# Dividing the attention shares of two mixing layers on ScalarE instead of GpSimd

## The chip, the cores and the metric

The kernel runs on one core of one Trainium2 chip. The metric is the device time of one execution in microseconds (us), the median of several executions; lower is better. A core has TensorE (PE in the profile, its weight loads apart as PEld), VectorE (DVE), ScalarE (ACT), GpSimd (POOL) and SyncE (SP), each with its own in-order instruction stream; they meet at semaphores.

## The reference, cut to what matters

Two transformer blocks run one after the other on 256 tokens of width 1024, all in float32. The second block prepends 16 meta tokens (272 rows in all) and has two layers; each has a mixing part with an attention branch and a convolution branch, then a feed-forward part. The attention branch is what the change touches:

```python
def sink_softmax(s, sink):
    m = jnp.maximum(jnp.max(s, -1, keepdims=True), sink)
    p = jnp.exp(s - m)
    return p / (jnp.sum(p, -1, keepdims=True) + jnp.exp(sink - m))
# one head: scores of a tile of queries, plus a bias table, masked
# p = sink_softmax(concat(s_meta, s_band), sink); o = p @ v
...
# the other branch, from the same projection u of the layer's input
h = val * sigmoid(gate); h = causal depthwise conv of width 31 (h) + db
y_conv = silu(layer_norm(h)) @ w_conv_proj
mix = (sigmoid(u_ga) * (attention @ w_attn_proj) + sigmoid(u_gc) * y_conv) @ w_out
```

There are 8 query heads of 64 and 2 key heads, a window of 128, and an attention sink per head. The "shares" are `p` after the division by its row sum.

## The kernel before, in words

Weights stream from HBM as 308 units of 16 tiles of 128x128. SyncE issues their loads into a ring of four staging buffers (`stg`). ScalarE rounds a unit to a high part (`wh`, line 1239), VectorE subtracts to get the low part (`wl`, line 1745); both rings hold three units. A matrix product is three matmuls per tile: high by high, high by low, low by high (lines 538 to 540 for tiles of 272 or 256 columns). The splits are written into the ScalarE and VectorE streams at each unit's boundary, for the unit two ahead.

Each engine's program is one Python function (`tensor_program`, `scalar_program`, `vector_program`, `gpsimd_program`, `sync_program`), and each has its own `mix_layer(l)` for the two mixing layers l = 0 and 1. In that stage TensorE computes 30 column tiles `nt` of the input projection (`u` and `g`), one after the other, 24 matmuls each. The evacuation of a tile is `evac(nt)` on ScalarE and VectorE; on TensorE, `pump(nt)` stands behind the tile's matmuls. From `nt` = 13 on (`FIRST_STEP`) every `evac` and `pump` also carries two steps of the attention. A job is one head and one tile of queries: 24 jobs in layer 0, in turns of two jobs of 16 queries and 16 keys, two of 128 queries and 144 keys, two of 128 and 272; 16 jobs in layer 1, without the 16-query ones. Step i of an engine does, where the job exists:

- TensorE (`pump`, `step`): for even i the product of shares and values of jobs i-8 and i-7 (`values`, line 819, which waits for `turned_p` of job i-7); for even i the scores of jobs i and i+1 (line 835); then the transposes of the shares of job i-5 (line 845, `DEEP` = 5), which wait for the shares of that job.
- VectorE (`front`, `back`): `front` adds the bias to the scores in PSUM, takes the maximum with the sink and writes the logits to one of five SBUF buffers `L` (line 2084). It also waits until job i-5, which had that buffer, is transposed. `front` of both jobs comes first, then three taps of the convolution (line 2109), then `back` of both jobs, the reciprocal of the row sum (line 2091), which waits for the exponential; then the rest of the taps due and, at a unit's boundary, the split.
- ScalarE (`step`): copies the transposed shares of job i-5 from PSUM to SBUF (line 1484), then the exponential of job i in place, with its row sum (line 1491), and, for every last job of a pair of heads, the high part of the attention output (lines 1498 and 1499).
- GpSimd (`step`): waits for the reciprocal of job i and multiplies the job's `L` by it, in place (line 2589).

So the order of the work is written out by hand, an order per engine; nothing is planned at run time. The taps of the convolution must all be done before TensorE sums them (`conv_sums`, line 881), which it does after the first tile of the attention's output projection. Then a layer norm over the convolution and an activation run through VectorE and ScalarE, before the next projection can end.

PSUM has eight banks, handed out in turn; a bank is used again once what was in it has been read.

Of the kernel before, what the change touches and what calls it, by code (L numbers as in the profile page):

```python
# [11 lines left out]
ALU = mybir.AluOpType  # L12
ACT = mybir.ActivationFunctionType
# [4 lines left out]
KD = D // P  # L18
# [141 lines left out]
DEEP = 5  # L160
BEHIND = DEEP + 2
FIRST_STEP = 13
# [29 lines left out]
def model_kernel(nc, first_d, w_d, x_d, meta_d, small_d, const_d, look_d, out_d):  # L192
# [3 lines left out]
    with ctx:  # L196
# [10 lines left out]
        m = Marks(handle)  # L207
# [46 lines left out]
        for l in range(2):  # L254
            c = MIXER[l]
            with ExitStack() as st:
# [3 lines left out]
                    TH=sb(f"TH{l}", [P, c["HT"], S], F32R, st), TL=sb(f"TL{l}", [P, c["HT"], S], F32R, st),  # L260
                    L=[sb(f"Lm{l}{i}", [P, c["NK"]], F32, st) for i in range(c["ring"] - 1)] + [flat(XC)[:, 1024:1024 + c["NK"]]],
                    PT=[sb(f"PTm{l}{i}", [P, c["NCH"], P], F32, st) for i in range(2)]
                    + [flat(SQ)[:, 1024:1024 + c["NCH"] * P].rearrange("p (c n) -> p c n", n=P)],
                    z=sb(f"zm{l}", [P, c["ring"] + 2, 8], F32, st)))
# [3 lines left out]
        for l in range(2):  # L268
            with ExitStack() as st:
                both = sb(f"H{l}", [P, 32, 2, S], F32R, st)  # L270
                ffn.append(dict(H=both, HH=both[:, :, 0, :], HL=both[:, :, 1, :],
                                t=[sb(f"ft{l}{i}", [P, S], F32, st) for i in range(3)], u=[sb(f"fu{l}{i}", [P, S], F32, st) for i in range(3)]))
        mix2 = []
        for l in range(2):
            with ExitStack() as st:
# [4 lines left out]
                    SG=sb(f"SG{l}", [P, 2, KD, T], F32, st), MH=sb(f"MH{l}", [P, KD, T], F32R, st), ML=sb(f"ML{l}", [P, KD, T], F32R, st),  # L280
                    ns=sb(f"ns{l}", [P, 8], F32, st), L=[sb(f"Lb{l}{i}", [P, T + 1], F32, st) for i in range(DEEP)],
                    PT=[sb(f"PTb{l}{i}", [P, 3, P], F32, st) for i in range(3)], z=sb(f"zb{l}", [P, DEEP + 2, 8], F32, st)))
# [104 lines left out]
        JOBS2 = [band_jobs(0), band_jobs(1)]  # L387
# [26 lines left out]
        def tensor_program(w, pe):  # L414
# [205 lines left out]
            def turn_pair(tag, a, i, j, last):  # L620
# [3 lines left out]
                for g in range(0, len(ch), 4):  # L624
# [3 lines left out]
                    for c, (k, wide, _) in enumerate(four):  # L628
                        ins = pe.transpose(PS[b][:, c * P:(c + 1) * P], a["L"][i % len(a["L"])][:, k:k + wide], ident)
                    ins.then_inc(*m.inc("group", ("turn", tag, i, g)))  # L630
# [169 lines left out]
            def mix_layer(l, st):  # L800
                a, jobs = mix2[l], JOBS2[l]
                lo = 0 if l == 0 else M
                n = T - lo
                tag, done, scored, opened = f"b{l}", [0], [], {}
# [20 lines left out]
                def step(i):  # L825
                    if i % 2 == 0 and 0 < i - BEHIND < len(jobs):
                        values(i - BEHIND)
                    if i % 2 == 0 and i < len(jobs):
                        if i == 0:
                            w.wait_ge(*m.of("key_zero", l))  # L830
                            w.wait_ge(*m.of("u_out", (l, 12)))
                        bs = [bank(("score", tag, i + k), ("biased", (tag, i + k))) for k in range(2)]
                        for (b, old), j in zip(bs, jobs[i:i + 2]):
                            vacant(old)
                            pe.matmul(PS[b][0:j["nq"], 0:j["nk"] + 1], j["q"], j["k"], start=True,
                                      stop=True).then_inc(*m.inc("group", ("score", tag, len(scored))))
                            scored.append(b)
                    t = i - DEEP
                    if 0 <= t < len(jobs):
                        nq, ch = jobs[t]["nq"], jobs[t]["chunks"]  # L840
                        w.wait_ge(*m.of("shares", (tag, t)))
                        b, old = bank(("turn", tag, t, 0), *[("turned_p", (tag, t, 0, n0)) for _, n0, _, _ in runs_of(ch, nq)])
                        vacant(old)
                        for c, (k, wide, _) in enumerate(ch):
                            ins = pe.transpose(PS[b][0:wide, c * P:c * P + nq], a["L"][t % DEEP][0:nq, 1 + k:1 + k + wide], ident[0:nq, 0:nq])
                        ins.then_inc(*m.inc("group", ("turn", tag, t, 0)))
                        m.also("group", ("turn", tag, t))
# [372 lines left out]
        def scalar_program(w, act):  # L1220
# [249 lines left out]
            def mix_layer(l):  # L1470
                a, jobs = mix2[l], JOBS2[l]
                lo = 0 if l == 0 else M
                tag, done = f"b{l}", [0]

                def step(i):
                    t = i - DEEP
                    if 0 <= t < len(jobs):
                        nq = jobs[t]["nq"]
                        w.wait_ge(*m.of("group", ("turn", tag, t)))
                        if t >= 3:  # L1480
                            w.wait_ge(*m.of("group", ("pair", tag, (t - 3) // 2 * 2 + 1)))
                        for _, n0, n1, wide in runs_of(jobs[t]["chunks"], nq):
                            dst, src = a["PT"][t % 3][0:wide, n0:n1, 0:nq], bank(("turn", tag, t, 0))[0:wide, n0 * P:n1 * P]
                            act.activation(dst, src.rearrange("p (a b) -> p a b", b=P)[:, :, 0:nq], ACT.Copy).then_inc(*m.inc("turned_p", (tag, t, 0, n0)))
                        m.also("turned_p", (tag, t, "all"))
                    if i < len(jobs):
                        j, z = jobs[i], a["z"][:, i % (DEEP + 2), :]
                        nq, nk = j["nq"], j["nk"]
                        L = a["L"][i % DEEP][0:nq, 0:nk + 1]
                        w.wait_ge(*m.of("biased", (tag, i)))  # L1490
                        act.activation(L, L, ACT.Exp, bias=z[0:nq, 0:1], scale=-1.0, accum_out=z[0:nq, 3:4]).then_inc(*m.inc("exp", (tag, i)))
                    v = i - BEHIND
                    if 0 < v < len(jobs) and v % 2 and jobs[v]["tt"] == 1:
                        hp = jobs[v]["hp"]
                        src, dst = bank(("pair", tag, hp)), a["MH"][:, hp, :]
                        w.wait_ge(*m.of("group", ("pair", tag, v)))
                        if l == 0:
                            act.activation(dst[:, 0:M], src[:, 0:M][:, ::-1], ACT.Copy).then_inc(*m.step("meta_high"))
                        act.activation(apart(dst[:, M:T]), in_turn(src[:, M:T]), ACT.Copy).then_inc(*m.inc("x_high", (f"a{l}", hp)))
# [984 lines left out]
        def gpsimd_program(w, pool):  # L2484
            def walk(NT, KT, evac=None):
                for nt in range(NT):
                    if evac is not None:
                        evac(nt)
# [90 lines left out]
                        pool.tensor_tensor(SQ[:, 0, :], SQ[:, 0, :], SQ[:, kt, :], ALU.add).then_inc(*m.inc("sq_added", (name, kt)))  # L2579

            def mix_layer(l):
                a, jobs, tag, done = mix2[l], JOBS2[l], f"b{l}", [0]

                def step(i):
                    if i < len(jobs):
                        j, z = jobs[i], a["z"][:, i % (DEEP + 2), :]
                        L = a["L"][i % DEEP][0:j["nq"], 1:1 + j["nk"]]
                        w.wait_ge(*m.of("recip", (tag, i)))
                        pool.tensor_scalar(L, L, z[0:j["nq"], 4:5], None, ALU.mult).then_inc(*m.inc("shares", (tag, i)))

                def evac(nt):
                    if nt >= FIRST_STEP:
                        for _ in range(2):
                            if done[0] < len(jobs) + BEHIND:
                                step(done[0])
                                done[0] += 1

                w.wait_ge(*m.of("group", ("y1", KD - 1) if l == 0 else ("dn", KD - 1)))
                pool.memset(a["HC"][:, :, 0:30], 0.0).then_inc(*m.inc("pad_zero", l))
                pool.memset(a["KT"][:, 0:1], 0.0).then_inc(*m.inc("key_zero", l))  # L2600
                pool.tensor_copy(a["BB"][0][:, :, 0], small("sinks", l * 8, 8)).then_inc(*m.inc("sink_in", (l, 0)))
                pool.tensor_copy(a["BB"][1][:, :, 0], small("sinks", l * 8, 8)).then_inc(*m.inc("sink_in", (l, 1)))
                pool.tensor_copy(a["BM"][:, :, 0], small("sinks", l * 8, 8)[0:M]).then_inc(*m.inc("sink_in", l))
                toeplitz(a["BB"][1][:, :, 1 + M:1 + T], 40, 8, 127, S, P, f"band_in{l}", 0)
                toeplitz(a["BB"][1][:, :, 1:1 + M], 48, 8, 271 - 144, M, P, f"band_in{l}", 1)
                toeplitz(a["BB"][0][:, :, 1 + M:1 + M + P], 40, 8, 127 + P, P, P, f"band_in{l}", 2)
                toeplitz(a["BB"][0][:, :, 1:1 + M], 48, 8, 271 - 16, M, P, f"band_in{l}", 3)
                toeplitz(a["BM"][:, :, 1:1 + M], 48, 8, 271, M, M, f"band_in{l}", 4)

                walk(30, KD, evac)  # L2610
                walk(KD, 4)
                walk(KD, 4)
                walk(KD, KD, lambda nt: running(f"o{l}", f"n1{l}", nt))

            w.wait_ge(*m.of("consts_in"))
# [160 lines left out]
```

## Time and profile before

| | |
|---|---|
| median of 3 runs | 1641.17 us (1640.95 to 1641.51) |
| profiled execution: its own time | 1641.93 us |
| profiled execution: span of the core | 1640.1 us |
| TensorE busy | 1614.9 us, 98% of the span |
| VectorE, ScalarE, GpSimd busy | 76%, 59%, 19% |
| granted TensorE clock | 1.00 (2.4 GHz) |
| attention of mixing layer 0 | 702 to 755 us of the span |
| attention of mixing layer 1 | 1081 to 1126 us of the span |

The span is what the profiler saw of the core; the execution's own time is 1.8 us longer. Busy shares are averages over stages with different limits, so a stage is read by itself, and there by what ended each wait.

### The profile page before, as it was taken

The numbers are of one execution on the slowest core, as the hardware profiler recorded it, in microseconds if no ns is written. First come the engines' busy times: TensorE is split into PE (matmuls) and PEld (weight loads), VectorE is DVE, ScalarE is ACT, GpSimd is POOL, SyncE is SP. The second block draws the span as 40 slices with busy tenths as digits, with TensorE's granted clock in tenths as the row PEclk, the third lists the DMA queues.
The fourth block names the chain that finished last, engine by engine and source line by source line (L and its number), as shares of the span: only waits on it lengthen the run. The fifth ranks groups of instructions, "written<-read, shape, count | busy, mean of one in ns | idle before, by whom it ended". The sixth has DMA issues, their size and how long they took to land.

```text
span 1640.1 us, 27535 instructions
## 1 busy us (share of the span) xinstructions
PE 1614.9 (98%) x11024; PEld 1472.9 (90%) x11024; DVE 1240.9 (76%) x1770; ACT 968.3 (59%) x1379; POOL 304.4 (19%) x301
## 2 busy tenths in 40 slices
PE   9999999999999999999999999999999999999997
PEld 8988888898888889989999999999988888888886
DVE  6565776666567656998975545899988898998897
ACT  6556674346657634555554433555568677776775
POOL 1230652123236302052300002131210000000000
PEclk9999999999999999999999999999999999999999
DMA  9732555563245546432435554534439898988983
GB/s 336 254 121 86 180 189 189 187 230 131 103 180 183 202 163 227 154 142 103 167 142 180 180 180 172 180 129 151 159 132 339 328 346 342 338 336 331 353 339 125
DMA packets 50740, 340.78 MB, mean 208 GB/s; under 512 B 5611, under 2 KB 7819, under 8 KB 11184
## 3 DMA queue, kind: packets, MB, share of 16 engines
q1 hardware_dynamic: 47920, 329.83, 54.9%
q0 software_dynamic: 2544, 9.12, 1.8%
q8 instruction: 90, 1.47, 0.4%
q14 instruction: 42, 0.34, 0.1%
q10 hardware_dynamic: 144, 0.01, 0.0%
HBM read 337.81 MB, written 1.13 MB: 207 GB/s over the span
## 4 chain that ended last, share of the span: by engine, by line
PE 86%; DVE 4%; issue 3%; ACT 3%; POOL 2%; DMA 1%; SPq 0%; POOLq 0%; DVEq 0%; ACTq 0%
PE bank L564 12%; PE bank L538 8%; PE bank L540 8%; PE bank L539 8%; PE bank L562 7%; PE bank L994 5%; PE bank L995 5%; PE bank L996 5%; PE bank L1027 2%; PE bank L1026 2%; PE bank L1025 2%; PE bank L691 2%; PE bank L693 2%; PE bank L692 2%; PE bank L444 1%
## 5 line engine op out<-in xcount | busy, mean ns | idle before, releaser
L1745 DVE TENSOR_TENSOR wl<-stg,wh 128x2048 fp32r<-128x2048 f32 x308 | 708.0, 2302 | 206.9 <-ACT wh L1239 204.2
L1239 ACT ACTIVATE wh<-stg 128x2048 fp32r<-128x2048 f32 x308 | 588.9, 1912 | 181.0 <-PE bank L996 81.3
L538 PE MATMUL bank<-xx,wh 128*128 128x272 f32 (+1 forms) x778 | 225.3, 290 | 0.0
L540 PE MATMUL bank<-xx,wl 128*128 128x272 f32 (+1 forms) x778 | 223.1, 287 | 0.0
L539 PE MATMUL bank<-xx,wh 128*128 128x272 f32 (+1 forms) x778 | 223.0, 287 | 0.0
L564 PE MATMUL bank<-xx,wh 128*128 128x512 f32 x448 | 159.7, 396 | 0.0
L564 PE MATMUL bank<-H,wh 128*128 128x512 f32 x434 | 151.3, 390 | 0.0
L994 PE MATMUL bank<-wh,GH 128*128 128x512 f32 (+3 forms) x400 | 147.5, 369 | 0.0
L539 PEld LDWEIGHTS bank<-xx,wh 128*128 128x128 f32 x778 | 147.4, 190 | 0.0
L538 PEld LDWEIGHTS bank<-xx,wh 128*128 128x128 f32 x778 | 146.4, 188 | 1.1 <-issue 0.7
L540 PEld LDWEIGHTS bank<-xx,wl 128*128 128x128 f32 x778 | 146.3, 188 | 0.0
L995 PE MATMUL bank<-wh,GL 128*128 128x512 f32 (+3 forms) x400 | 146.3, 366 | 0.0
L996 PE MATMUL bank<-wl,GH 128*128 128x512 f32 (+3 forms) x400 | 146.3, 366 | 0.0
L691 PE MATMUL bank<-wh,xx 128*128 128x256 f32 x480 | 139.3, 290 | 2.1 <-DVE xx L1793 1.1
L693 PE MATMUL bank<-wl,xx 128*128 128x256 f32 x480 | 134.8, 281 | 0.0
L692 PE MATMUL bank<-wh,xx 128*128 128x256 f32 x480 | 134.5, 280 | 0.0
L562 PE MATMUL bank<-xx,wl 128*128 128x256 f32 x512 | 132.4, 279 | 0.0
L562 PE MATMUL bank<-H,wl 128*128 128x256 f32 x448 | 123.9, 282 | 0.0
L2549 POOL TENSOR_TENSOR fu<-ft 128x256 f32<-128x256 f32 x64 | 85.2, 1334 | 132.3 <-ACT ft L1390 132.3
L2109 DVE SCALAR_TENSOR_TENSOR CA<-HC,small,CA 128x272 f32<-128x272 f32 x240 | 107.5, 500 | 0.7
L562 PEld LDWEIGHTS bank<-xx,wl 128*128 128x128 f32 x512 | 96.5, 188 | 5.9 <-issue 0.3
L564 PEld LDWEIGHTS bank<-xx,wh 128*128 128x128 f32 x448 | 84.1, 188 | 17.2
(385 smaller groups left out, 3545.1 us busy)
## 6 DMA issues: line engine op xcount, KB each, us to landing
stg<-in_w SPq DMA_DIRECT2D x308, 1024.0 KB, 4.9
BT<-bias_scratch POOLq DMA_DIRECT2D x3, 1024.0 KB, 9.7
stg<-in_first SPq DMA_DIRECT2D x4, 512.0 KB, 6.1
stg<-in_w SPq DMA_DIRECT2D x4, 512.0 KB, 9.4
BT<-bias_scratch POOLq DMA_DIRECT2D x1, 2048.0 KB, 12.0
BB<-bias_scratch POOLq DMA_DIRECT2D x2, 1024.0 KB, 6.6
res<-in_x SPq DMA_DIRECT2D x1, 1024.0 KB, 8.8
BB<-bias_scratch POOLq DMA_DIRECT2D x2, 512.0 KB, 7.2
```

The lines of the kernel that those rows point to most:

```text
L538: pe.matmul(out, wh, xh(kt), start=kt == 0, stop=False)
L539: pe.matmul(out, wh, xl(kt), start=False, stop=False)
L540: ins = pe.matmul(out, wl, xh(kt), start=False, stop=kt == KT - 1)
L562: ins = pe.matmul(PS[b][:, 0:S], wl, high(kt), start=False, stop=False)
L564: ins = pe.matmul(out, wh, both(kt), start=False, stop=kt == KT - 1)
L691: pe.matmul(out, xh_t(kt, tt), wh, start=kt == 0, stop=False)
L693: ins = pe.matmul(out, xh_t(kt, tt), wl, start=False, stop=kt == KD - 1)
L994: pe.matmul(out, lh(kt, i), wh, start=kt == 0, stop=False)
L995: pe.matmul(out, ll(kt, i), wh, start=False, stop=False)
L996: ins = pe.matmul(out, lh(kt, i), wl, start=False, stop=kt == KD - 1)
L1239: act.activation(WH[u % NW][:, :], stg[place(u)][:, :], ACT.Copy).then_inc(*m.inc("w_high", u))
L1745: vec.tensor_tensor(WL[u % NW][:, :], stg[place(u)][:, :], WH[u % NW][:, :].bitcast(F32), ALU.subtract).then_inc(*m.inc("w_low_v", u))
```

## The change

The division leaves GpSimd's program and enters ScalarE's, in `step`, as an activation `Copy` with the reciprocal as its scale per partition, in place. It stands ahead of everything else in step i and divides job i-2, where GpSimd divided job i as soon as its reciprocal was there. TensorE's transposes wait for the new semaphore. GpSimd keeps the rest of `mix_layer`: its two fills, three small copies and five loads of bias tables at the layer's start, and the running sums at its end.

```diff
@@ tensor_program, mix_layer, step
-                        w.wait_ge(*m.of("shares", (tag, t)))
+                        w.wait_ge(*m.of("mixed_shares", (tag, t)))
@@ scalar_program, mix_layer
                 def step(i):
+                    d = i - 2
+                    if 0 <= d < len(jobs):
+                        nq = jobs[d]["nq"]
+                        L = a["L"][d % DEEP][0:nq, 1:1 + jobs[d]["nk"]]
+                        w.wait_ge(*m.of("recip", (tag, d)))
+                        act.activation(L, L, ACT.Copy, scale=a["z"][0:nq, d % (DEEP + 2), 4:5]).then_inc(*m.inc("mixed_shares", (tag, d)))
                     t = i - DEEP
                     if 0 <= t < len(jobs):
...
@@ gpsimd_program
             def mix_layer(l):
-                a, jobs, tag, done = mix2[l], JOBS2[l], f"b{l}", [0]
-
-                def step(i):
-                    if i < len(jobs):
-                        j, z = jobs[i], a["z"][:, i % (DEEP + 2), :]
-                        L = a["L"][i % DEEP][0:j["nq"], 1:1 + j["nk"]]
-                        w.wait_ge(*m.of("recip", (tag, i)))
-                        pool.tensor_scalar(L, L, z[0:j["nq"], 4:5], None, ALU.mult).then_inc(*m.inc("shares", (tag, i)))
-
-                def evac(nt):
-                    if nt >= FIRST_STEP:
-                        for _ in range(2):
-                            if done[0] < len(jobs) + BEHIND:
-                                step(done[0])
-                                done[0] += 1
-
+                a = mix2[l]
...
-                walk(30, KD, evac)
-                walk(KD, 4)
-                walk(KD, 4)
                 walk(KD, KD, lambda nt: running(f"o{l}", f"n1{l}", nt))
```

## Rows read from the trace of the kernel before

**Rows 1.** The page, first part: busy us, share of the span, instructions.

```profile
PE 1614.9 (98%) x11024; PEld 1472.9 (90%) x11024; DVE 1240.9 (76%) x1770; ACT 968.3 (59%) x1379; POOL 304.4 (19%) x301
```

**Rows 2.** Stretches (start:end, length, PE, PEld, DVE, ACT, POOL, clock, DMA, GB/s): both attentions.

```profile
702.00:755.00 53.00, 53.00 (x444) 46.20 (x444) 49.07 (x141) 33.12 (x105) 33.62 (x24) 1.00 0.34 121
1081.00:1126.00 45.00, 45.00 (x393) 38.80 (x393) 43.82 (x114) 29.64 (x86) 21.27 (x16) 1.00 0.38 134
```

**Rows 3.** Waits of the weight loads, 695 to 770 us: total us, times, longest.

```profile
PEld bank L845 <- POOL Lb L2589: 0.7, 3, 0.4
```

**Rows 4.** Timeline of ScalarE, layer 1: start us, us, what [idle before <-releaser].

```profile
1084.86 0.51 ACT L1491 ACTIVATE Lb<-Lb,zb 128x273 f32<-128x273 f32 x1
...
1089.28 0.42 ACT L1491 ACTIVATE Lb<-Lb,zb 128x145 f32<-128x145 f32 x1 [3.42 <-DVE zb L2084]
...
1090.01 0.40 ACT L1491 ACTIVATE Lb<-Lb,zb 128x145 f32<-128x145 f32 x1
1090.41 1.90 ACT L1239 ACTIVATE wh<-stg 128x2048 fp32r<-128x2048 f32 x1
1092.22 0.35 ACT L1518 ACTIVATE SG<-bank 128x256 f32<-128x256 f32 x1
1092.47 0.41 ACT L1484 ACTIVATE PTb<-bank 16x128 f32<-16x128 f32 x2
...
1093.72 0.51 ACT L1491 ACTIVATE Lb<-Lb,zb 128x273 f32<-128x273 f32 x1
```

**Rows 5.** Timeline of ScalarE, layer 0, the copy of job 1.

```profile
711.64 0.16 ACT L1484 ACTIVATE PTb<-bank 16x16 f32<-16x16 f32 x1
```

**Rows 6.** Timeline of VectorE, layer 1.

```profile
1082.60 0.89 DVE L2109 SCALAR_TENSOR_TENSOR CA<-HC,small,CA 128x272 f32<-128x272 f32 x2
...
1085.63 1.13 DVE L2109 SCALAR_TENSOR_TENSOR CA<-HC,small,CA 128x272 f32<-128x272 f32 x2
...
1094.35 0.16 DVE L2091 RECIPROCAL zb<-zb 128x1 f32<-128x1 f32 x1 [0.33 <-ACT Lb L1491]
1094.43 1.02 DVE L2109 SCALAR_TENSOR_TENSOR CA<-HC,small,CA 128x272 f32<-128x272 f32 x2
1095.36 2.29 DVE L1745 TENSOR_TENSOR wl<-stg,wh 128x2048 fp32r<-128x2048 f32 x1
...
1115.50 3.74 DVE L2109 SCALAR_TENSOR_TENSOR CA<-HC,small,CA 128x272 f32<-128x272 f32 x8
...
1122.52 3.38 DVE L2109 SCALAR_TENSOR_TENSOR CA<-HC,small,CA 128x272 f32<-128x272 f32 x8
1126.84 0.42 DVE L2099 TENSOR_TENSOR ML<-bank,MH 128x256 fp32r<-128x256 f32 x1 [0.94 <-ACT MH L1499]
...
1136.90 5.16 DVE L2109 SCALAR_TENSOR_TENSOR CA<-HC,small,CA 128x272 f32<-128x272 f32 x12
```

**Rows 7.** The chain that ended last, layer 1: start us, us, what.

```profile
1093.20 0.73 PE bank L819 x8
...
1112.75 0.73 PE bank L819 x8
...
1142.23 1.83 PE bank L881 x8
```

**Rows 8.** The chain, layer 0, the product of jobs 0 and 1.

```profile
713.21 0.22 PE bank L819 x4
```

**Rows 9.** Timeline of VectorE, layer 0: its `front` rows behind an idle time.

```profile
719.50 0.50 DVE L2084 CUSTOM_DVE_ANT_0 Lb<-bank,BB,ns 128x273 f32<-128x273 f32 x1 [0.92 <-PE bank L845]
...
747.57 0.50 DVE L2084 CUSTOM_DVE_ANT_0 Lb<-bank,BB,ns 128x273 f32<-128x273 f32 x1 [1.46 <-PE bank L845]
```

**Rows 10.** Timeline of GpSimd, layer 1.

```profile
1099.63 1.50 POOL L2589 TENSOR_SCALAR Lb<-Lb,zb 128x144 f32<-128x144 f32 x2 [1.23 <-DVE zb L2091]
1102.37 0.96 POOL L2589 TENSOR_SCALAR Lb<-Lb,zb 128x272 f32<-128x272 f32 x1 [1.24 <-DVE zb L2091]
...
1112.60 3.82 POOL L2589 TENSOR_SCALAR Lb<-Lb,zb 128x272 f32<-128x272 f32 x2 [1.74 <-DVE zb L2091]
```

## The prediction, made before the changed kernel ran

> **What bounds the kernel now.** I read the page's busy shares first, then the two attention stretches one by one, then what TensorE waits for in them, and last the timelines of ScalarE and VectorE. TensorE is busy 98% of the span at 2.4 GHz [rows 1]. In both attention stretches it is busy throughout, 53.00 of 53 and 45.00 of 45 us, at a granted clock of 1.00; beside it VectorE has 3.9 and 1.2 us left, ScalarE 20 and 15 [rows 2]. So the reader is to see that there is next to nothing to win: the shares that GpSimd makes never stop a matmul. The only trace of them is 0.7 us in three gaps of the weight loads, 0.4 us the longest, while the matmuls ran on [rows 3]. What the change can do is mostly harm, or nothing. The place to look is the margin by which ScalarE and VectorE are in time, in layer 1 above all, where VectorE is 97% busy.
>
> **The prices.** Removed: 24 and 16 multiplications of GpSimd, 33.6 and 21.3 us of it [rows 2], off the path. Nothing is queued behind them but the running sums at the layer's end, which wait for later results; GpSimd's loads of bias tables were issued at the layer's start, so no DMA moves. Added: as many activations on ScalarE. The trace has no such one, so I take the exponential of the same buffer, which is in place too and has one operand per partition: 0.40 us for 145 columns and 0.51 for 273, of which some 0.09 overlaps with the next instruction (the split of 1090.41 lasts 1.90, the next row starts 1.81 later) [rows 4]. That is 0.31 and 0.42 us of ScalarE's time for a share. From below, the tanh of 256 columns holds the engine 0.25 us (1092.22 to 1092.47); from above, 0.40 and 0.51 without overlap [rows 4]. For 16x16, the copy's 0.16 less overlap to 0.2 [rows 5]. Layer 1: 8 x 0.31 + 8 x 0.42 = 5.8 us; layer 0: 8 x 0.2 more, 7.4 us. That ScalarE has this time free does not hide it: it counts where it stands in front of something urgent.
>
> **The new wait.** ScalarE waits for the reciprocal of job i-2, which VectorE made in its evacuation of the column tile before. VectorE cannot reach the logits of job i before it has made that reciprocal, and ScalarE needs those logits two instructions later anyway; so this wait costs nothing of its own. What counts is the order behind it. In step i the share stands ahead of the copy of job i-5, which TensorE's product needs at its next tile; in step i+1 it stands between the two exponentials of the pair, and VectorE's second reciprocal, with its taps, split and next logits queued behind it, waits for the second exponential.
>
> **Layer 1, followed along the rows.** (1) Shares 0 and 1 push exponential 3 by 2 x 0.31; it ended at 1085.46 (1084.86 + 0.51 and its row sum), now about 1086.1. VectorE's reciprocal waits for it, so VectorE goes on with its two taps about 0.5 us later than 1085.63, and gets 0.24 back, because these taps take 1.13 us beside GpSimd and 0.89 undisturbed [rows 4, 6]. Next logits: +0.3. ScalarE had idled 3.42 us for them at 1089.28, so it too is +0.3 there. Then share 3 (0.42) stands before exponential 5: +0.7 at the split of 1090.41. Share 4 (0.31) stands before the copy of job 1: +1.0. The copy ended at 1092.88; now 1093.9. TensorE started the product of jobs 0 and 1 at 1093.1 (weights; 1093.20 in the chain) [rows 4, 7]. **A stall of 0.8 us.**
> (2) From here the loop logits, exponential, share, copy, exponential, reciprocal, taps, split, logits closes on ScalarE and VectorE. In the two tiles that belong to one weight unit it holds four shares, two of each size, 1.46 us, of which VectorE gets 0.1 to 0.3 back per group of taps (1.02 against 0.89 at 1094.43) and some was slack (VectorE waited only 0.33 us at 1094.35) [rows 6]. Adding instruction by instruction, VectorE's split that began at 1095.36 comes 1.2 us later, the one after 2.1, the one after 3.1. The product of jobs 8 and 9, at 1112.75 before, is due at 1113.5 with the first stall in it; its copy is ready at 1113.8: **another 0.3 to 0.4 us.** The product between those two is in time by some 0.2 us.
> (3) With the last job the loop ends. VectorE gets back 0.36 us at 1115.50, where eight taps took 3.74 us beside GpSimd and 3.38 later, and the 0.94 us that it idled at 1126.84; that leaves 3.1 - 0.4 - 0.9 = 1.8 us at its last taps, which ended at 1136.90 + 5.16 = 1142.06. TensorE's sums of the convolution wait for these and started at 1142.23 [rows 6, 7]: 0.17 us of margin. So they start 1.6 us later, of which 1.15 were lost before and **0.4 to 0.5 are a third stall.** Behind them the layer norm runs in series, so nothing gives it back. Layer 1: **+1.6 us.**
> The weights are no new wait: a split stands two units (19 us; a unit is (1112.75 - 1093.20) / 2 = 9.8) ahead of its use, and is at most 3.1 us late; SyncE's load of the unit four ahead starts as much later, with the same cover.
>
> **Layer 0.** The first margin is larger: the copy of job 1 ended at 711.80, the product started at 713.2 [rows 5, 8]; shares 2 to 4 take about 1.0 us of 1.4. Later VectorE idles for TensorE's transposes, 0.92 us at 719.5 and 1.46 at 747.6 [rows 9]. The lag, 1 to 2 us by the same addition, dies in these, and the smallest margin of a product that I find is 0.2 us. **0 for layer 0**, between -0.7 (if the gaps of [rows 3] were true waits) and +1.
>
> **Sum.** +1.6 us on the profiled execution's own 1641.93, the span of 1640.1 and 1.8 around it. That execution is 0.8 us above the median of the runs shown, so I put the sum on the median: 1641.17 + 1.6 = **1642.8**. With shares at the lower price (0.25) the first stall shrinks to 0.3 and the whole to 0.8; at the upper one it is 2.6.
>
> **A rule against my credit.** In the rows two taps take 0.13 to 0.25 us longer beside GpSimd, while GpSimd's pair of 272 columns, at most 2 x 0.96 us undisturbed, takes up to 3.82: it is GpSimd that mostly waits [rows 6, 10]. The Trainium skill, "SBUF — State Buffer", section "Who interferes with whom", has an instruction of VectorE with two SBUF inputs, as the taps, contend with one of GpSimd that reads SBUF, as an exclusive lock: whoever comes second is fully blocked. If in layer 1 VectorE were the blocked one each time, it would get back up to 8 x 0.75 + 8 x 0.96 = 13.7 us [rows 10] instead of 1.3, its lag would be gone, and only the first stall could remain: the first rival. The trace agrees that the two contend, not that VectorE is the loser.
>
> **Rivals.** *Hidden:* the shares are cheaper or VectorE, rid of GpSimd, gains more than I credit; the copy of job 1 still comes within 0.3 us of its time. For it: ScalarE is idle a third of the stretch. Against: the idle time lies before the logits, not before the copy. Time: 1641.2, or 0.7 less if the gaps of [rows 3] go; 1640.5 to 1641.9. *The loop becomes the bound (slower):* exponential, share, copy, exponential and VectorE's 97% are one ring, and if nothing absorbs it every share of layer 1 is paid in full: 5.8 - 1.3 = 4.5 us, 1645.7, or more if layer 0's idle times do not absorb theirs (7.4 more at the very worst). It decides from the point where the ring takes longer than TensorE's 9.8 us per unit for more than the two units that layer 1 has; my addition has it at about 10.3, so it is close, but short. *Faster by over 3.3 us:* TensorE has no 3 us of idle time in either stretch [rows 2], so only a shorter chain behind the convolution could do it, and this is not touched. *It doesn't do what it says:* a `Copy` already stands between exponentials here without anything loaded in between [rows 4], so no new function table; I leave nothing for that.
>
> **How the numbers follow.** Forecast (+0.8 to +3.2): 0.57. Hidden: 0.26. Loop: 0.14. Faster by over 0.2%: 0.03. What a measurement can tell from no change is about 0.2%, 3.3 us, so forecast and hidden are both "within": 0.83, slower 0.14, faster 0.03. The range runs from 1640.7, near the hidden case's lower end, to 1645.2, into the loop's: one in ten left above, some five in a hundred below. The forecast's own range is 1642.0 to 1644.4.
>
> **What would show it.** In the profile after: GpSimd without work in both stretches; forty activations of 0.3 to 0.5 us on ScalarE's new line; taps in pairs back at 0.89 us. Steps 1 and 2: TensorE waiting at line 819 for ScalarE's copy in layer 1, once near 1093 for about 0.8 us and once 20 us later, none in layer 0. Step 3: a wait of line 881 for VectorE's taps. VectorE's waits at line 2091, as the 0.33 us of 1094.35, grown to some 4 us in all in layer 1. Wrong, if no line of TensorE waits in layer 1, if line 845 waits for ScalarE, or if layer 0 stalls.

## The result, and the profile after

The changed kernel takes 1645.26 us (median of 11 runs, 1644.48 to 1646.69) against 1641.16 (1640.94 to 1641.54) for the kernel before beside it: ratio 1.0027 [1.0018, 1.0035], 4.1 us slower. That is outside the predicted range by 0.06 us, and well off the predicted 1642.8. Six of the 11 runs lie at 1644.48 to 1645.26 and five at 1646.11 to 1646.69; the profiled execution (1646.69, span 1644.9) is of the second group. The recorded mean of TensorE's granted clock is 0.999 in each of the six and 0.998 in each of the five.

The page after: busy time by engine, and the first line of the chain of waits. [rows 1] is the first of them before. GpSimd lost 54 us, ScalarE gained 12 in 40 more instructions, VectorE none; TensorE is "busy" 3 us longer with as many matmuls.

```profile
PE 1618.1 (98%) x11024; PEld 1475.9 (90%) x11024; DVE 1241.4 (75%) x1770; ACT 980.0 (60%) x1419; POOL 250.4 (15%) x261
...
PE 77%; DVE 9%; ACT 5%; issue 4%; POOL 2%; DMA 1%; SPq 0%; POOLq 0%; DVEq 0%; ACTq 0%
```

Where the time went is read by laying TensorE's timelines over each other. Two lines are good posts: 855, at the start of each attention, and 881, behind the convolution. First before (start us, us, what [idle before <-releaser]):

```profile
701.51 0.49 PE L855 MATMUL bank<-consts,VF 128*128 128x128 f32 x3
701.93 0.52 PE L835 MATMUL bank<-K,Q 64*128 64x145 f32 x4
...
727.36 0.62 PE L835 MATMUL bank<-K,Q 64*128 64x145 f32 x4
...
768.64 2.00 PE L881 MATMUL bank<-CA,consts 128*128 128x272 f32 x8
...
1081.26 0.49 PE L855 MATMUL bank<-consts,VF 128*128 128x128 f32 x3
...
1103.63 0.52 PE L835 MATMUL bank<-K,Q 64*128 64x145 f32 x4
...
1142.07 2.00 PE L881 MATMUL bank<-CA,consts 128*128 128x272 f32 x8
```

The same of the changed kernel:

```profile
701.39 0.49 PE L855 MATMUL bank<-consts,VF 128*128 128x128 f32 x3
...
727.24 0.51 PE L835 MATMUL bank<-K,Q 64*128 64x145 f32 x2
729.06 0.51 PE L835 MATMUL bank<-K,Q 64*128 64x145 f32 x2 [1.31 <-DVE ML L2105]
...
771.77 2.00 PE L881 MATMUL bank<-CA,consts 128*128 128x272 f32 x8
...
1084.38 0.49 PE L855 MATMUL bank<-consts,VF 128*128 128x128 f32 x3
...
1097.23 0.80 PE L819 MATMUL bank<-PTb,V 16*64 16x128 f32 x8 [0.90 <-ACT PTb L1490]
...
1107.74 0.94 PE L835 MATMUL bank<-K,Q 64*128 64x145 f32 x4
...
1118.63 0.38 PE L845 MATMUL bank<-consts,Lb 128*16 128x128 f32 x2 [0.20 <-DVE ML L2105]
...
1146.95 2.00 PE L881 MATMUL bank<-CA,consts 128*128 128x272 f32 x8
```

From 855 to 881, layer 0 took 67.13 us before (768.64 - 701.51) and takes 70.38: **+3.25**. Layer 1 took 60.81 and takes 62.57: **+1.76**. What lies between the two (881 to the next 855) is 312.62 and 312.61 us. The whole difference is in the two attentions, and the larger part in the one that was forecast at nothing.

**Layer 0.** TensorE's scores of job 15 wait for a PSUM bank, with 1.31 us of idle time in front of them. It held the first finished pair of heads, and it is free once VectorE has subtracted that pair's low part (`back`, line 2105; 2099 before). VectorE's timeline, before:

```profile
727.01 0.40 DVE L2099 TENSOR_TENSOR ML<-bank,MH 128x256 fp32r<-128x256 f32 x1
```

and after, with the three taps that stand in front:

```profile
727.22 1.31 DVE L2115 SCALAR_TENSOR_TENSOR CA<-HC,small,CA 128x272 f32<-128x272 f32 x3
...
728.60 0.40 DVE L2105 TENSOR_TENSOR ML<-bank,MH 128x256 fp32r<-128x256 f32 x1
```

Before, the subtraction ended at 727.41 (727.01 + 0.40), just after TensorE had started on these scores. All four matmuls are in one row at 727.36, but this row is 0.62 us long, and 0.52 where nothing is waited for (701.93; the same row in experiments 4 and 8). So the bank was already about 0.1 us late before the change: there was no margin at all. After, the subtraction starts 27.21 us behind line 855 instead of 25.50, so it is 1.71 us later, and so are the transposes behind the scores (729.50 against 727.91, each from its line 855). Then something that no term of the prediction had. The stretches of one us each that follow (start:end, length, busy us and count of PE, PEld, DVE, ACT, POOL, granted clock, DMA share, GB/s):

```profile
728.00:729.00 1.00, 0.00 (x0) 0.00 (x0) 1.00 (x6) 1.00 (x6) 0.00 (x0) 1.00 0.82 139
729.00:730.00 1.00, 0.94 (x8) 0.78 (x8) 0.96 (x5) 1.00 (x1) 0.00 (x0) 1.00 0.94 393
730.00:731.00 1.00, 1.00 (x7) 1.00 (x6) 1.00 (x6) 1.00 (x3) 0.00 (x0) 0.61 1.02 434
731.00:732.00 1.00, 1.00 (x7) 1.00 (x6) 1.00 (x5) 1.00 (x6) 0.00 (x0) 0.50 0.22 90
732.00:733.00 1.00, 1.00 (x6) 1.00 (x6) 0.39 (x3) 0.91 (x5) 0.00 (x0) 0.50 0.00 0
733.00:734.00 1.00, 1.00 (x8) 1.00 (x7) 1.00 (x3) 0.00 (x0) 0.00 (x0) 0.68 0.00 0
734.00:735.00 1.00, 1.00 (x10) 0.72 (x9) 1.00 (x1) 0.21 (x1) 0.00 (x0) 1.00 0.00 0
```

TensorE stood still in 728 to 729; a little more than a us after it was back at work its granted clock fell to 0.50, 1.2 GHz, for some three us. In TensorE's timeline its matmuls of 272 columns are there 0.23 us apart instead of 0.125, fifteen of them: 15 x 0.10 = 1.5 us. "PE busy" hides this: it reads 1.00 throughout the slow stretch. So 3.25 = 1.71 by which the bank is late and 1.5 of clock. The idle time of 1.31 is 0.4 short of the 1.71, because two of these matmuls fill a row as long as four do (0.51 against 0.52): what the profile counts as busy behind job 14's scores is time in which job 15's would have run beside them. The Trainium skill, "TensorE: Matmul & The Clock Gate", "Part 1: The HAM clock gate", has these two levels, and says of a kernel's start that the number of matmuls at the lower one differs from run to run of one kernel. Here too executions of one kernel differ in it, as the mean clocks of the two groups show (and experiment 6).

**Layer 1.** Three delays. The first is a wait of 0.90 us at the product of jobs 0 and 1, for ScalarE's copy. The second is at 1107.74, where the row of the scores is 0.94 long instead of 0.52. That is the bank again: the scores of job 13 need the one that this layer's first pair of heads held, and they start at 1108.16, right behind VectorE's low part (the timelines of VectorE and, from 1108.3 on, of TensorE):

```profile
1107.69 0.42 DVE L2105 TENSOR_TENSOR ML<-bank,MH 128x256 fp32r<-128x256 f32 x1
...
1108.16 0.51 PE L835 MATMUL bank<-K,Q 64*128 64x145 f32 x2
```

The list of TensorE's waits does not have it, since job 12's matmuls count as busy meanwhile. The third is at 1118.63, 0.20 us of idle time, again for a bank that VectorE's low part frees. By the later starts they make 0.98 + 0.42 + 0.37 = 1.77 us.

ScalarE's timeline shows the shares themselves (line 1481); [rows 4, 5] are its rows before.

```profile
730.89 0.29 ACT L1481 ACTIVATE Lb<-Lb,zb 16x16 f32<-16x16 f32 x1
...
1087.48 0.40 ACT L1481 ACTIVATE Lb<-Lb,zb 128x144 f32<-128x144 f32 x1
1087.79 0.51 ACT L1497 ACTIVATE Lb<-Lb,zb 128x273 f32<-128x273 f32 x1
...
1092.85 0.42 ACT L1497 ACTIVATE Lb<-Lb,zb 128x145 f32<-128x145 f32 x1 [2.98 <-DVE zb L2090]
...
1093.27 0.51 ACT L1481 ACTIVATE Lb<-Lb,zb 128x272 f32<-128x272 f32 x1
1093.68 0.41 ACT L1490 ACTIVATE PTb<-bank 16x128 f32<-16x128 f32 x2
```

The first share holds the engine 0.31 us (1087.48 to 1087.79), the one at 1093.27, directly ahead of the copy that TensorE waits for, 0.41. ScalarE idled 2.98 us shortly before: this idle time was no cover, as it lay on the wrong side of the logits.

### The profile page after: what moved, and what is told of

The parts are those of the page before. It is cut to its first block, busy times and chain, and to the rows that moved or that the text cites. A ratio compares the mean times of both kernels' runs of the same rounds, so it can differ in the third digit from the quotient of the medians.

```text
span 1644.9 us, 27535 instructions
## 1 busy us (share of the span) xinstructions
PE 1618.1 (98%) x11024; PEld 1475.9 (90%) x11024; DVE 1241.4 (75%) x1770; ACT 980.0 (60%) x1419; POOL 250.4 (15%) x261
## 3 DMA queue, kind: packets, MB, share of 16 engines
HBM read 337.81 MB, written 1.13 MB: 206 GB/s over the span
## 4 chain that ended last, share of the span: by engine, by line
PE 77%; DVE 9%; ACT 5%; issue 4%; POOL 2%; DMA 1%; SPq 0%; POOLq 0%; DVEq 0%; ACTq 0%
PE bank L564 12%; PE bank L562 7%; PE bank L538 6%; PE bank L540 6%; PE bank L539 6%; PE bank L994 5%; PE bank L996 5%; PE bank L995 5%; DVE wl L1751 3%; PE bank L1027 2%; PE bank L1026 2%; PE bank L1025 2%; DVE CA L2115 2%; PE bank L691 2%; ACT wh L1239 2%
```

## The experiments

All have the kernel before beside them (1641.20 beside experiments 1 to 4, 1641.28 beside the others). Each has 11 runs, experiment 3 five. Beside the median I give, from each profiled execution, the two stretches from line 855 to 881, as above; this takes out what happens elsewhere. That is needed: of the ten profiled executions five reach line 855 of layer 0 at 700.7 to 700.9 us and five, those of before and after among them, at 701.4 to 701.7. The cause lies far ahead of the attention and stays open.

| kernel | median us | ratio | layer 0 | layer 1 |
|---|---|---|---|---|
| before | 1641.16 | | 67.13 | 60.81 |
| after | 1645.26 | 1.0027 [1.0018, 1.0035] | +3.25 | +1.76 |
| 1 only layer 0 | 1644.83 | 1.0018 [1.0009, 1.0027] | +3.32 | 0.00 |
| 2 only layer 1 | 1643.47 | 1.0015 [1.0006, 1.0025] | +0.01 | +1.75 |
| 3 idle copies | 1647.29 | 1.0035 [1.0021, 1.0048] | +2.05 | +2.39 |
| 4 no shares | 1641.36 | 1.0000 [0.9991, 1.0009] | -0.10 | 0.00 |
| 5 early low part | 1643.24 | 1.0012 [1.0003, 1.0021] | +0.25 | +1.75 |
| 6 filled wait | 1644.92 | 1.0022 [1.0013, 1.0031] | +1.84 | +1.73 |
| 7 both shares late | 1643.56 | 1.0013 [1.0004, 1.0022] | +1.26 | +0.86 |
| 8 = 5 and 7 | 1642.62 | 1.0007 [0.9998, 1.0016] | -0.10 | +0.86 |

**1. Only layer 0 changed.** GpSimd divides in layer 1 as before.

```diff
-                        w.wait_ge(*m.of("shares", (tag, t)))
+                        w.wait_ge(*m.of("mixed_shares" if l == 0 else "shares", (tag, t)))
...
+                    if l == 0 and 0 <= d < len(jobs):
...
+                if l != 0:
+                    walk(30, KD, evac)
```

> Only layer 0's 24 shares move to ScalarE; layer 1's 16 stay on GpSimd. My theory: in layer 0 the shares lengthen the ring of VectorE and ScalarE, VectorE is 1.3 us late with the low part of the first attention output (near 728 us of the span), and TensorE's scores of job 15 wait for the PSUM bank that this part still occupies; in about half of the executions the granted clock falls for some 3 us behind that wait and costs another 1.7. So 1.2 to 1.5 us over the kernel before in some executions, 2.9 to 3.3 in the others, nothing in layer 1. Rival (layer 1, which has the tighter margins, carries the loss, and the rest is noise): under 0.5 us.

Layer 0 costs 3.32 us alone, with the same wait (below: total us, times, longest) and the same fall of the clock (stretch 730 to 733):

```profile
PE bank L835 <- DVE ML L2105: 1.4, 1, 1.4
```

```profile
730.00:733.00 3.00, 3.00 (x17) 2.98 (x16) 2.60 (x10) 3.00 (x11) 0.00 (x0) 0.55 0.47 197
```

Its times too fall into two groups, 1642.97 to 1643.38 (four runs) and 1644.40 to 1645.76 (seven), 1.8 to 2.2 and 3.2 to 4.6 us over the kernel before, which is more than the 1.2 to 1.5 and 2.9 to 3.3 expected. Five of the seven have a mean granted clock of 0.997, below the four's 0.998; the other two do not, so the clock does not explain them.

**2. Only layer 1 changed.** The same with `l == 1`.

> Only layer 1's 16 shares move; layer 0's stay on GpSimd. My theory, as in the forecast's steps for layer 1: a stall of about 0.9 us at the first product of shares and values, 0.2 us at the transposes, and late convolution taps; together 1.6 to 1.9 us, in every execution, without a fall of the clock. With the run of layer 0 alone it adds up to the whole, 4.1 us. Rival (the two layers' delays are not independent): the two runs sum to under 3 or over 5 us.

Layer 1 costs 1.75 us, with the waits of the changed kernel there; layer 0 has none. The stretches add up (3.32 + 1.75 = 5.07, against 5.01 together). The medians do not (3.6 + 2.3 = 5.9 against 4.1, past the 5 that was to speak for the rival). Two things part them: in both, the time outside the span is 0.3 to 0.5 us longer, which I can't explain; and the median of experiment 1 lies in its longer group, that of the change in its shorter one. The runs of experiment 2 spread from 2.0 to 3.6 us over the kernel before, where 1.6 to 1.9 in every execution was expected.

**3. The shares stay on GpSimd, ScalarE makes as many copies for nothing**, into a spare tile, at the same places and behind the same waits.

```diff
+                    d = i - 2
+                    if 0 <= d < len(jobs):
+                        nq, nk = jobs[d]["nq"], jobs[d]["nk"]
+                        w.wait_ge(*m.of("recip", (tag, d)))
+                        if d:
+                            w.wait_ge(*m.of("spare", (tag, d - 1)))
+                        act.activation(a["spare"][0:nq, 0:nk], CS[0:nq, 0:nk], ACT.Copy, scale=small("gains", 0)[0:nq, :]).then_inc(*m.inc("spare", (tag, d)))
```

> The kernel before, GpSimd dividing as before, and on ScalarE at the same places 40 activations of the same shapes that copy a constant into a spare tile nobody reads (with the wait for the same reciprocal). Nothing waits for them. My theory (ScalarE's time in the ring is the cost, not the new owner of the shares): 4 to 5.5 us over before, a little more than the change, since VectorE still meets GpSimd; waits at the lines of the scores and of the product in the same places. Rival (the handover of the shares is the cost: TensorE's transposes wait for a later producer): within 0.7 us of before.

The stalls of the changed kernel are there at the same places, though no one needs the copies (lines are one further on TensorE, two on VectorE; first layer 0, then layer 1):

```profile
PE bank L836 <- DVE ML L2107: 1.6, 1, 1.6
...
PE bank L820 <- ACT PTb L1492: 1.2, 1, 1.2
PE bank L846 <- DVE ML L2107: 0.3, 1, 0.3
```

What costs is ScalarE's time in the ring of ScalarE and VectorE, not that the division changed hands. The stalls are larger than in the changed kernel, which fits that GpSimd still slows VectorE's taps (a mean of 502 ns in layer 0 against 492), though no run shows this by itself. In layer 0 the wait is longer and the total smaller: the clock was 1.00 all through in this execution. So the cost there is the lateness of the low part alone, 27.54 us behind line 855 (700.83) against 25.50 before, 2.04 later:

```profile
728.37 0.40 DVE L2107 TENSOR_TENSOR ML<-bank,MH 128x256 fp32r<-128x256 f32 x1
```

```profile
730.00:733.00 3.00, 3.00 (x26) 2.85 (x27) 2.38 (x11) 2.69 (x12) 0.67 (x2) 1.00 0.31 128
```

The time missed its forecast, 6.1 us over the kernel before by the median instead of 4 to 5.5; the five runs are 1645.88, 1646.18 (the profiled one) and 1647.29 to 1647.47, and whether the clock parts them is not shown.

**4. No division at all.** TensorE's transposes wait for the exponential; the shares stay undivided (the changed kernel without its new lines on ScalarE).

```diff
-                        w.wait_ge(*m.of("mixed_shares", (tag, t)))
+                        w.wait_ge(*m.of("exp", (tag, t)))
```

> The division is left out altogether, on GpSimd and on ScalarE; the transposes wait for the exponential alone. My theory (GpSimd's shares were never on the path, and VectorE's relief from GpSimd is worth nothing to TensorE): -0.7 to +0.3 us against before. Rival (GpSimd's contention with VectorE was costing time): faster by 1 us or more.

Nothing, 1.0000, and no waits of TensorE's matmuls in either attention. The 0.10 us in layer 0 is the bank's small wait of before, which is gone. Otherwise the division on GpSimd cost the kernel before no time, so there was next to nothing to gain.

**5. The change, with the low part of layer 0 made early:** ScalarE's high part first in its step, VectorE's subtraction ahead of `front`.

```diff
+                    v = i - BEHIND
+                    if l == 0 and 0 < v < len(jobs) and v % 2 and jobs[v]["tt"] == 1:
+                        hp = jobs[v]["hp"]
...
-                    if 0 < v < len(jobs) and v % 2 and jobs[v]["tt"] == 1:
+                    if l == 1 and 0 < v < len(jobs) and v % 2 and jobs[v]["tt"] == 1:
```

> The changed kernel, but in layer 0 ScalarE takes the high part of a finished attention output ahead of its share, and VectorE the low part ahead of the next logits instead of behind the taps; so the PSUM bank comes free some 2 us sooner. The shares stay on ScalarE, 40 of them. My theory (the wait for that bank, and the clock's fall behind it, are all of layer 0's loss): 1643.0 to 1643.6 in every execution, layer 1's 1.8 us being left; no wait at the scores' line in layer 0; clock 1.00 at 727 to 740. Rival (layer 0 loses time by ScalarE's lateness in general, and the bank is only where it shows first): another wait takes its place in layer 0 and the time stays above 1644.

Close to what was expected: +0.25 us in layer 0, clock 1.00, and layer 1 as in the changed kernel. The list of TensorE's waits has none in layer 0, but the row of the scores is 0.76 us long, for the low part ends at 726.93:

```profile
726.51 0.42 DVE L2095 TENSOR_TENSOR ML<-bank,MH 128x256 fp32r<-128x256 f32 x1
...
726.74 0.76 PE L835 MATMUL bank<-K,Q 64*128 64x145 f32 x4
```

That is 0.14 more than before; the other 0.1 is lost ahead of the next product. So with the bank free earlier nearly all of layer 0's cost goes, the fall of the clock with it: the bank is the cause there. Nine of 11 runs lie at 1642.98 to 1643.47, two at 1644.1 to 1644.3, above the forecast, with their cause open.

**6. The change, with the wait of layer 0 filled** by four matmuls of 256 columns ahead of the scores of job 14, into the bank that these scores then overwrite.

```diff
+                            for _ in range(4 if l == 0 and i == 14 and b == bs[0][0] else 0):
+                                pe.matmul(PS[b][:, 0:256], ones, CS[:, 0:256], start=True, stop=True)
```

> The changed kernel with four dummy matmuls of 256 columns (0.23 us each, one behind the other) put ahead of the scores of job 14 in layer 0, into the bank that these scores then overwrite: TensorE works through about 0.9 us of the wait for the bank. They add work and take away no wait. My theory (the executions that are 1.7 us longer than the others are those in which the granted clock fell behind TensorE's idle time): all executions at 1644.4 to 1645.3, as the shorter ones of the change, clock 1.00 near 730. Rival (the two groups of times have another cause): both groups stay, or all are longer by the 0.9 us added.

TensorE's timeline, and the stretch 730 to 733:

```profile
727.36 1.99 PE L836 MATMUL bank<-consts 128*128 128x256 f32 x8
729.29 0.52 PE L837 MATMUL bank<-K,Q 64*128 64x145 f32 x4
```

```profile
730.00:733.00 3.00, 3.00 (x27) 3.00 (x25) 2.45 (x10) 3.00 (x12) 0.00 (x0) 1.00 0.43 180
```

The four matmuls are eight in the trace and take 1.93 us, not the 0.9 expected, so they fill the whole wait. The scores of job 15 start 0.11 us later than in the changed kernel (729.29 behind a line 855 at 701.51, against 729.06 behind 701.39), and yet layer 0 is 1.41 us shorter, since the clock stays at 1.00. That measures the fall by itself: 1.5, as counted above. No run lies above 1645.73; the changed kernel's longer group, 1646.11 to 1646.69, is gone. Four of the 11, the profiled one (1645.67) among them, lie at 1645.41 to 1645.73, above the forecast's 1645.3; the clock is not seen to part these from the others, and their cause stays open.

**7. The change in another order:** the copy first in each step, and the shares of both jobs of a pair together, ahead of the next pair's first exponential.

```diff
-                    d = i - 2
-                    if 0 <= d < len(jobs):
...
+                    for d in (i - 2, i - 1) if i % 2 == 0 else ():
+                        if 0 <= d < len(jobs):
```

> The changed kernel with another order in ScalarE's step: the copy of the transposed shares first, then both shares of the pair before its first exponential (where ScalarE waits for logits anyway in every second tile), and none between the two exponentials. As many instructions on ScalarE. My theory (what counts is what stands behind the share, not the 13 us of ScalarE's time): the first product of layer 1 waits 0.1 to 0.3 us instead of 0.9, the reciprocals in layer 1 wait about 2.5 us instead of 3.6, layer 0's wait for the bank shrinks to under 0.7; 1642.0 to 1643.2. Rival (ScalarE's total time): as the change, 1644.5 or more.

Waits of TensorE in layer 0 and layer 1 (PEld: of its weight loads):

```profile
PE bank L835 <- DVE ML L2105: 0.9, 1, 0.9
...
PE bank L819 <- ACT PTb L1484: 0.2, 1, 0.2
...
PEld bank L835 <- DVE ML L2105: 0.4, 1, 0.4
```

In layer 1 the product is as expected: without a share ahead of the copy, 0.90 becomes 0.2. The scores there still wait for the bank; by the later starts this is 0.6 of the 0.86 that are left. The other figures missed: 1643.56 lies above the forecast's 1643.2 (though below the rival's 1644.5), the reciprocals in layer 1 wait 3.0 us, not 2.5, and layer 0 waits 0.9, not under 0.7. VectorE's low part there:

```profile
728.49 0.40 DVE L2105 TENSOR_TENSOR ML<-bank,MH 128x256 fp32r<-128x256 f32 x1
```

Line 855 starts at 701.73 in this execution, so the low part comes 26.76 us behind it, against 27.21 in the changed kernel and 25.50 before: the order takes off 0.45 of a lag of 1.71. The 1.26 that stay are what layer 0 costs, at a clock of 1.00.

**8. 5 and 7 together.** The edits as above.

> Both edits, the order of e7_both_first and the earlier low part of e5_early_low in layer 0. My theory: layer 0 loses nothing, layer 1 0.4 to 1.0 us: 1641.6 to 1642.4. Rival (the two repairs act on the same delay): no faster than the better one of the two. Neither theory has it below the kernel before by more than 0.5 us, as TensorE did not wait there.

0.2 us above what I expected, and by its interval not to be told apart from the kernel before (1.0007 [0.9998, 1.0016]). By the stretches all of layer 0's cost is gone and half of layer 1's. The rest there is the product's 0.2 and the bank's 0.6; the low part is early in layer 0 alone, and no run has it early in layer 1. No version beats the kernel before, and after experiment 4 none should.

## Why the prediction was wrong

**The failed step is "0 for layer 0".** It said that the lag of "1 to 2 us by the same addition" dies in VectorE's later idle times, and that the smallest margin of a product is 0.2 us. The lag was right (1.71 us at the low part), and nothing later in the layer is delayed by it. But I had gone through the products and the copies that they need, and not through TensorE's other waits on VectorE in that stretch: scores need a free bank, and that bank's last reader is a subtraction that `back` puts behind `front` and three taps. It had no margin, which could be read in rows that I had not looked at (727.01 and 727.36, shown above). Against the forecast of 0 this stretch cost 3.25 us, of which the bank's lateness is 1.71. Experiments 1, 5 and 8 settle that the bank is the cause.

**A term was missing.** A stall was priced at its length. Here a bank 1.71 us late cost 3.25, the other 1.5 by the granted clock, in the profiled execution and, by the times and mean clocks, in four of the ten others. [rows 2] had the clock at 1.00 in both stretches, and the trace before gave no sign of this term. It has a wait of TensorE as long, far ahead of the attention, and the clock is 1.00 all through 130 to 140 us:

```profile
134.59 0.87 PE L629 MATMUL bank<-consts,Lm 128*128 128x128 f32 x6 [1.41 <-POOL Lm L2513]
```

**Layer 1: sum right, two of three places wrong, so in part by luck.** Forecast +1.6, measured +1.76. Step 1 was right in place and size (0.8 at line 819; 0.90). Step 2 put 0.3 to 0.4 at the product of jobs 8 and 9; that one did not wait, and 0.42 came two tiles earlier, at the scores, for the bank that VectorE's low part frees: the kind of wait that was overlooked in layer 0. Step 3, 0.4 to 0.5 at line 881, did not come; 0.37 was lost before, at 1118.63, for a bank too. The 0.17 us of margin in step 3 was misread: line 881 sums four tiles one after the other in 2 us, and only the last sum needs the last taps. In the changed kernel it starts at 1146.95 without a wait, before these taps end (1142.01 + 5.17 = 1147.18). Of the prediction's signs of being wrong, a stall in layer 0 came. At line 845 only weight loads waited for a share of ScalarE; its one matmul that waited did so for VectorE. VectorE's last taps started 2.0 us later in the layer (1142.01 against 1136.90 [rows 6], less the 3.1 of layer 0) where 1.8 were forecast:

```profile
1085.72 0.90 DVE L2115 SCALAR_TENSOR_TENSOR CA<-HC,small,CA 128x272 f32<-128x272 f32 x2
...
1089.31 1.02 DVE L2115 SCALAR_TENSOR_TENSOR CA<-HC,small,CA 128x272 f32<-128x272 f32 x2
...
1142.01 5.17 DVE L2115 SCALAR_TENSOR_TENSOR CA<-HC,small,CA 128x272 f32<-128x272 f32 x12
```

So the lag of VectorE was forecast well, and how it reached TensorE was not; that steps 2 and 3 were to cost 0.7 to 0.9 and the two bank waits cost 0.8 is luck. VectorE's waits for the exponential, forecast at "some 4 us", are 3.6:

```profile
DVE zb L2097 <- ACT Lb L1497: 3.6, 5, 1.1
```

**Prices and credit.** 0.31 and 0.42 us a share were exact (0.31, 0.41), and 0.2 for the 16x16 too. The credit was too large: two taps take 1.02 us in the same place without GpSimd as well (1089.31, against the 1.13 of 1085.63 in [rows 6]), so only 0.11 of the 0.24 was contention. All 97 taps of layer 0, 690 to 770 us, took 43.8 us before and 42.9 after:

```profile
L2109 DVE SCALAR_TENSOR_TENSOR CA<-HC,small,CA 128x272 f32<-128x272 f32 x97 | 43.8, 500 | 0.2
```

```profile
L2115 DVE SCALAR_TENSOR_TENSOR CA<-HC,small,CA 128x272 f32<-128x272 f32 x97 | 42.9, 492 | 0.2
```

So the case in which VectorE is the one that the rule of the Trainium skill ("SBUF — State Buffer", "Who interferes with whom") blocks did not come: 24 multiplications of GpSimd, 33.6 us of them [rows 2], gave VectorE 0.9 us back when they went.

**The rivals.** *The loop becomes the bound* named 1645.7, near the result, by another way: it paid every share of layer 1, and layer 1 gave 1.76 of its 4.5. So its time was nearly met, its place not. *Hidden* falls with the result itself, *faster* also with experiment 4. Of the forecast's own case, without layer 0, experiments 2 and 5 are the nearest pictures: 1643.47 and 1643.24, inside its 1642.0 to 1644.4.

## What to carry to other kernels

When a stream of instructions will be late by some amount, list every wait of the bounding engine on it in the stretch, the freeing of PSUM banks too, and look for the one with the least margin before the next idle time; results that are needed for their values are only half of that list. A bank is freed by its last reader, and a reader that stands behind optional work (here three taps) makes an invisible deadline. Price such a delay by how late the awaited result is, not by the idle time that the profile counts, and leave room in the range for a fall of the clock behind it: here 1.5 us, in some executions and not in others.

## What the runs showed of the hardware

- After 1.31 and 1.4 us in which TensorE waited (the change, experiment 1), its granted clock was 0.50 for some three us from about one us after it was back at work, and matmuls of 272 columns came 0.23 us apart instead of 0.125. After 1.6 us (experiment 3) and 0.9 us (experiment 7) in the same place, and after 1.41 us at another (the kernel before), it stayed at 1.00. So the length of the wait alone did not decide; what does is open here.
- What TensorE lost at a clock of 1.00 was the lateness of what it waited for, and the idle time in the profile was some 0.4 us shorter: in layer 0 the low part was 2.04 us later in experiment 3 and 1.26 in experiment 7, the stretch 2.05 and 1.26 longer, and the idle time 1.6 and 0.9.
- An activation in place with one scale per partition took 0.29, 0.40 and 0.51 us for 16, 144 and 272 columns, and held ScalarE 0.1 us less.
